# Modulation weights multiplied in the pauses of the norms, a reordered modulated input and an earlier first gain

## What is computed

```
h = h + 0.5 * rmsnorm(swiglu(rmsnorm(h, g[0]), w_gu, w_down), g[1])
xn = rmsnorm(h, g[2]);  z = xn @ w_in            # mLSTM, spatial gating, cross attention, gates
h = h + rmsnorm((g0*(y_m@w0) + g1*(y_s@w1) + g2*(y_x@w2)) @ w_out, g[3])
h = h + 0.5 * rmsnorm(swiglu(rmsnorm(h, g[4]), w_gu2, w_down2), g[5])
```

## Time and profile before

| what | value |
|---|---|
| runs shown | 3615.26, 3619.67, 3625.52 us |
| execution that was profiled | 3617.66 us |
| its span, first to last instruction | 3615.5 us |
| mean granted TensorE clock | 0.944 |
| TensorE busy | 3258.3 us, 90% |
| VectorE busy | 1895.6 us, 52% |
| ScalarE busy | 1405.6 us, 39% |
| GpSimd busy | 356.6 us, 10% |

### The profile page before, as it was taken

How to read it: one execution, slowest core, us unless ns; L and a number is a source line. 1 busy time by engine, 2 the same in 40 slices (tenths; PEclk the granted TensorE clock), 3 DMA queues, 4 the chain that set the end, 5 groups by cost and what they waited for, 6 DMA issues and landing times.

```text
span 3615.5 us, 54646 instructions
## 1 busy us (share of the span) xinstructions
PE 3258.3 (90%) x22888; PEld 2787.4 (77%) x22888; DVE 1895.6 (52%) x2581; ACT 1405.6 (39%) x2037; POOL 356.6 (10%) x387
## 2 busy tenths in 40 slices
PE   7989999898998999989898689898899979896897
PEld 7878887697887788779676578886688868786795
DVE  4356645445445664544524666663333367576554
ACT  3345554335335544433522333331323244412443
POOL 2000000100100000010010233330000001033000
PEclk9999999899999999999999789998899989987999
DMA  9655545665765555476441000002232223500464
GB/s 266 213 155 167 165 150 177 205 210 173 246 197 159 163 170 151 160 235 198 145 127 41 1 2 8 2 3 82 72 99 94 88 71 88 146 1 12 135 180 133
DMA packets 449227, 459.77 MB, mean 127 GB/s; under 512 B 18288, under 2 KB 347184, under 8 KB 449008
## 3 DMA queue, kind: packets, MB, share of 16 engines
q1 hardware_dynamic: 428624, 385.08, 35.8%
q0 software_dynamic: 20384, 71.52, 5.9%
HBM read 455.50 MB, written 1.05 MB: 126 GB/s over the span
## 4 chain that ended last, share of the span: by engine, by line
PE 75%; DVE 15%; ACT 5%; issue 4%; DMA 1%; POOL 1%; DVEq 0%; ACTq 0%; SPq 0%; POOLq 0%
PE banks L311 20%; PE banks L312 19%; PE banks L313 19%; PE banks L1901 2%; DVE weights_lo L297 1%; PE banks L4275 1%; PE banks L3518 1%; PE banks L3520 1%; PE banks L3499 1%; PE banks L1287 1%; DVE arena L3921 1%; DMA arena<-in_ada_w 1%; DVE first_input_split L1298 1%; PE banks L4246 1%; DVE arena L1430 1%
## 5 line engine op out<-in xcount | busy, mean ns | idle before, releaser
L297 DVE TENSOR_TENSOR weights_lo<-raw_weights,weights_hi 128x1024 fp32r<-128x1024 f32 (+2 forms) x399 | 472.7, 1186 | 544.7 <-ACT weights_hi L289 470.4
L289 ACT ACTIVATE weights_hi<-raw_weights 128x1024 fp32r<-128x1024 f32 (+2 forms) x399 | 409.3, 1027 | 530.5 <-PE banks L313 525.0
L262 DVE TENSOR_TENSOR weights_lo<-raw_weights,weights_hi 128x1024 fp32r<-128x1024 f32 x180 | 220.8, 1228 | 472.8 <-ACT weights_hi L255 285.2
L255 ACT ACTIVATE weights_hi<-raw_weights 128x1024 fp32r<-128x1024 f32 x180 | 190.4, 1060 | 516.9 <-PE banks L313 511.5
L311 PE MATMUL banks<-first_input_split,weights_hi 128*128 128x256 f32 (+1 forms) x1218 | 357.9, 294 | 9.1 <-DVE first_input_split L1298 5.2
L313 PE MATMUL banks<-first_input_split,weights_lo 128*128 128x256 f32 (+1 forms) x1218 | 347.9, 286 | 0.0
L312 PE MATMUL banks<-first_input_split,weights_hi 128*128 128x256 f32 (+1 forms) x1218 | 346.9, 285 | 0.0
L297 DVE TENSOR_TENSOR third_weights_split<-raw_weights,third_weights_split 128x1024 fp32r<-128x1024 f32 (+1 forms) x173 | 207.1, 1197 | 233.3 <-ACT third_weights_split L289 190.9
L311 PE MATMUL banks<-work_split,weights_hi 128*128 128x512 f32 (+2 forms) x776 | 272.2, 351 | 24.0 <-DVEq L2405 20.2
L312 PE MATMUL banks<-input_split,weights_hi 128*128 128x512 f32 (+2 forms) x776 | 270.6, 349 | 0.0
L313 PE MATMUL banks<-work_split,weights_lo 128*128 128x512 f32 (+2 forms) x776 | 270.4, 349 | 0.0
(11 more groups left out here) (597 smaller groups left out, 7169.2 us busy)
## 6 DMA issues: line engine op xcount, KB each, us to landing
raw_weights<-in_w_ffn_gu SPq DMA_DIRECT2D x176, 512.0 KB, 4.7
raw_weights<-in_w_in SPq DMA_DIRECT2D x144, 512.0 KB, 3.7
raw_weights<-in_mlp_w SPq DMA_DIRECT2D x128, 512.0 KB, 3.9
arena<-in_ada_w POOLq DMA_DIRECT2D x96, 512.0 KB, 6.7
raw_weights<-in_w_ffn_down SPq DMA_DIRECT2D x80, 512.0 KB, 3.4
raw_weights<-in_w_branch SPq DMA_DIRECT2D x48, 512.0 KB, 3.6
raw_weights<-in_ssd_w_in SPq DMA_DIRECT2D x48, 512.0 KB, 3.9
raw_weights<-in_w_mkv SPq DMA_DIRECT2D x32, 512.0 KB, 4.2
```

Of the source, the lines that this page charges most:

```text
L255: last = s.activation(self.w_hi[:, u % 2, :], self.raw[:, u, :], ACT.Copy)
L262: last = v.tensor_tensor(self.w_lo[:, u % 2, :], self.raw[:, u, :], self.w_hi[:, u % 2, :].bitcast(F32), ALU.subtract)
L289: last = s.activation(hi, raw, ACT.Copy)
L297: last = v.tensor_tensor(lo, raw, hi.bitcast(F32), ALU.subtract)
```

## The change

Modulation pieces: nine slots beside the stream, each transfer also waits until the stream has come to where it was emitted (`c.multiplied`), 3, 3, 2 and 3 groups are multiplied beside the four feed-forwards (44 pieces), and 52 pieces are multiplied right behind the last matmul of a stream, ahead of the norms: 12, 8, 12, 12 and 8 pieces at five places. Three of each twelve are brought into the rows of the hidden activations that are used up, the eights into buffers of the mixing branches. The sums of up to three groups are then taken together, at the beginning of the next side generator, from banks 6 and 7; `normed_input` turns its rows in banks 0 to 3. The first gain is issued ahead of the constants, the second and third behind the memory. `modulated_input` is put in another order, and the first product of the hybrid mixer waits for its input tile by tile.

```diff
-MOD_SLOTS = 5
+MOD_SLOTS = 9
+MOD_ARRIVALS = 12
...
-            pe.wait_ge(self.steps_done, at)
+            pe.wait_ge(self.steps_done, at - 1 if tiles_made else at)
...
         def product(banks, u, hi, lo, pe):
             for n, t in enumerate(tiles):
+                if waits:
+                    pe.wait_ge(*waits.pop(0))
...
-        feature_major(c, ch, c.y[:, t, :], x, t, 4 + 2 * t)
+        feature_major(c, ch, c.y[:, t, :], x, t, 2 * t)
...
-    mod_rows, pick = cols(z, GATES, 2, SEQ), cols(c.small, 448, 2, 2)
+    mod_rows, pick = cols(z, LD_AT + P, 3, SEQ), cols(c.small, 448, 2, 2)
...
+    def bring_modulation_weights(at, *free):
...
+            if used or m >= MOD_ARRIVALS:
+                g.wait_ge(c.mods_multiplied, max(used + [m - MOD_ARRIVALS]) + 1)
+            g.dma_start(cols(z, at, 2, BANK), src).then_inc(c.mods_arrived[m % MOD_ARRIVALS], 16)
...
+    def modulation_sums():
...
+        count = pieces // UNITS - first
...
+        @c.block.scalar
+            for i in range(count):
+                last = s.activation(mod_rows[:, i, :], c.ps[:, 6 + i // 2, i % 2 * SEQ:(i % 2 + 1) * SEQ], ACT.Copy)
...
+    def modulation_groups(beside, ahead):
+        free = [chain_end(ch) for ch in c.tile + [c.side]]
+        first, end = c.mods_brought, c.mods_brought + UNITS * beside + ahead
+
+        def bring_some():
+            while c.mods_brought < min(end, c.mod_pieces + MOD_SLOTS):
+                at = MOD_AT + (c.mods_brought - first) % MOD_SLOTS * UNIT
+                bring_modulation_weights(at, (c.multiplied, c.units_split - 1), *(free if at == MOD_AT else ()))
+                yield
+                yield
+        for _ in range(beside):
+            for u in range(UNITS):
+                yield from bring_some()
+                multiply_modulation()
+                yield
+            yield from modulation_sums()
+        yield from bring_some()
+
+    def more_modulations(stream, count):
+        rows = stream.todo[-1][0]
+        for i in range(count):
+            bring_modulation_weights(i * UNIT, (c.lo_made, rows.numbers[4 * i + 3] + 1 + UNITS))
...
+        for i in range(4):
+            bring_modulation_weights(V_TOK + i * UNIT, chain_end(ch))
...
-    slots[0].fill(g[0, 0, :])
-    slots[1].fill(g[0, 1, :])
-    slots[2].fill(g[0, 2, :])
...
     bring_memory()
+    slots[1].fill(g[0, 1, :])
+    slots[2].fill(g[0, 2, :])
...
+        memory = itertools.chain(modulation_sums(), memory_input(layer), params_needed() if layer == 0 else (),
+                                 modulation_groups(3 - layer, MOD_SLOTS + 3))
...
+        more_modulations(stream, 3)
+        multiply_modulations()
         stream = mixing
         add_normed(c, done, slots[1], 0.5)
...
+    try_root(c)
+    if stream:
+        stream.split_ahead(2)
+    else:
+        c.split_first_weights()
+    first = min(tiles, 3)
+    for t in range(first):
+        squared(t, chains[t])
+    for t in range(first):
+        normed(t, chains[t])
+    modulated(0, chains[0])
+    for t in range(first, tiles):
+        squared(t, chains[t])
+        normed(t, chains[t])
+    for t in range(1, tiles):
+        modulated(t, chains[t])
+        parts(t - 1, chains[t - 1])
+    parts(tiles - 1, chains[tiles - 1])
+    c.tiles_made = chain_ends(chains)
...
+        c.slots[0].fill(a["norm_g"][0, 0, :])
         make_constants(c)
```

## The result

The changed kernel takes 3567.68 us at the median of four runs (3559.80 to 3571.59), beside 3621.03 us of the kernel before: a ratio of 0.9854, with a 95% interval of 0.9835 to 0.9873. It is 53 us faster than before, and 30 us slower than I forecast. The profiled execution took 3568.06 us, its span is 3566.3 us against 3615.5: 49.2 us of the 81.4 that my sum had.

What follows compares the result with a forecast made beforehand. TensorE, busy 90% of the span, was taken as the bound. Terms 39.5 + 2 + 12.8 + 5.1 + 6 + 3 + 13 = 81.4 us left 3536.3 of the profiled 3617.7; with 2 us for the median, 3538 us, range 3518 to 3566.

Steps and rivals of the forecast that it cites:

- 52 pieces out of the streams: Feed-forward streams: 52 of 96 pieces, 0.76 us each, move into pauses that hide them; 39.5 us saved.
- sums, at full clock: Small matmuls of 24 groups: 13 groups batched in five, one restart per batch; 2 us saved, bounds 0 to 4.
- stalls in the feed-forwards: Start of each feed-forward: TensorE's waits for the first piece vanish because nine are issued ahead; 12.8 us saved.
- clock in the product stages: First block's products: less time at 1.2 GHz, 5.1 us behind first pieces plus 6 us behind pauses.
- start: Kernel start: first gain issued earlier brings the first matmul forward; 3 us saved, bounds 1.5 and 4.
- first modulated input: Ahead of the second block's first product: reordered tiles save 4 us, taking input tile by tile 3 us; 7 in all.
- The overrun rival: Pauses: the clock falls within them, twelve pieces take 12 or 13 us and delay transposes; 3560 us, chance 0.17.
- the modulated inputs: Four modulated inputs: new order and tile-by-tile start save 7, 4, 2 and 0.4 us; 13 in all, bounds 7 and 17.
- The slower rival: Feed-forwards: pieces reach TensorE before their weights, 44 stalls of 3.2 us; 3692 us, chance 0.03.
- I take 6 us from the three twelves and nothing from the eights: Products behind the five pauses: filled pauses recover 6 us of clock loss behind twelve pieces, none behind eight; bounds 0 and 15.
- The 5.1 us behind the first pieces: Feed-forwards: removing first-piece stalls recovers 1.7 us of lowered clock behind each of three; 5.1 us saved.
- The row at 634.53: Profile row: a 2.89 us pause, transposes and another 2.05 us pause sufficed for a low clock; cited against full clock recovery.

Runs made afterwards that it cites:

- the control: The changed kernel once more with only an empty line added, nothing altered: 3560.23 us, ratio 0.9834 to the kernel before.
- the slower pace: Changed kernel with a piece beside a stream emitted every one and a half weight units instead of every unit: 3549.10 us, ratio 0.9811.
- the combination: Changed kernel plus identity transposes at both idle places of the pauses, sums some five units later, a piece every one and a half units: 3532.31 us, ratio 0.9770.

## Why the prediction was right and wrong

All in the first block, the spans of before against those of the changed kernel; the term of the pieces is what is left of the 37.5 us when the others are taken out, so an error of any other term of the product stages lies in it too:

| term | forecast | measured | read from |
|---|---|---|---|
| 52 pieces out of the streams | 39.5 | 41.4, or 0.80 each | remainder; 42 by the feed-forwards of the kernel with all pieces in the streams (37.0, plus 9.1 of clock and 0.8 of idle, less 4.5 of sums) |
| sums, at full clock | 2 | -0.7 | 24 x 0.81 = 19.4 before, 11 single ones (8.9) and 11.2 after |
| stalls in the feed-forwards | 12.8 | 7.8 | idle 21.0 us before, 13.2 after |
| idle in the mixings | 0 | -0.4 | 19.35 and 19.7 |
| clock in the product stages | 11.1 | -10.6, in the control -7.3 | half of 71.4 - 50.2, or of 64.7 - 50.2 |
| pauses | 0 | 0.3 | five 1.1 shorter, one 0.8 longer |
| start | 3 | 2.1 | 19.80 to 17.69 |
| first modulated input | 7 | 10.7 | 30.19 to 19.49 |
| sum, first block | 75.4 | 50.6 | 1816.74 to 1766.17 |
| second block | 6.4, taken as 6 in the sum | -1.4, in the control 5.5 | 1798.8 to 1800.1 or 1793.2 |

*Right.* The pieces: both the price in a stream and that the pause hides them. The overrun rival is out, with 2.1 to 3.5 us left behind the pieces in the changed kernel, though the time that it forecast, 3560 us, is what the control measured: that is a coincidence. The wait for first pieces went whole. By the distances from last to first product the modulated inputs gave 16.1 us where I had 13, the first 10.7 of it; the stream behind the first got only 0.6 us longer (143.8 to 144.4), so its early start is nearly all gain. The start gave 2.1, inside its bounds and nearer to the 2 us that I had worked out beside my 3 by the Trainium skill ("DMA: Bandwidth & Descriptors", Queues, rings and completion order). The slower rival did not come: no piece is late.

*Wrong, and the step of it.* "I take 6 us from the three twelves and nothing from the eights; bounds 0 and 15". The term of the clock is 22 us off, most of the 25 missing in the first block. Some 16 of them lie behind the three twelves, where 9.7 us more are missing instead of 6 less (17.2 against 7.5). The sign lay outside my bounds: I took it for certain that more work in a pause can only help. The 5.1 us behind the first pieces can't be told apart in this sum: those stalls are gone, but the stall at 944.94 has a low stretch of its own. The run with all pieces in the streams and the three with filled pauses show what holds. What counts for the next stream is where in time the clock falls. Twelve pieces of 5.4 us put off the fall from 3 to 5 us behind the last product to 9, so that the next stream bears it. The 2 us of idle between the transposes and the first product, which I named and left alone, decide. The row at 634.53, from which I argued that the clock would hardly come back, was the right row; I drew from it only that the gain would be small. The Trainium skill ("TensorE: Matmul & The Clock Gate", Part 1) has it that the low clock is the default and activity lifts it. With both idle stretches filled the traces agree (1.00 in five windows of the combination); a pause filled with twelve pieces only, with 2 to 3 us left empty on both sides of the transposes, came out worse than an empty one (17.2 us missing behind three, against 5.0 or 7.5).

*Also mis-sized.* The batches of sums: emitted "in the first two units of the next stream", two of them stand in just that low stretch and take 4.97 us each instead of 2.6, and at full clock a batch of 24 costs 2.6, so nothing is saved beside three times 0.81. The stalls: I had "nine units lie between issue and use" for the pieces, and did not ask what nine pieces issued at 2.87 us each do to the weights beside them. One stall of 3.34 us with 3.4 us at 1.2 GHz behind it is what shows, and the slower pace gives 8 to 16 us. The rest, 7 us in the second block of the first profile, is variation between executions.

*Luck.* The first measurement lies 2 us above my range and the control, the same kernel, 6 us inside it. That second number says nothing for the reasoning: the clock term had the wrong sign in both profiles, and the range was wide enough to hide it.

*Open.* Whether the small matmuls themselves bring the clock down (the falls behind three batches of 24) was not tried alone: in the combination, with the batches five units later, there was none behind them, with more filling there were two again, and with the batches late and no filling there was one. The first feed-forward also gains 4.4 us from the slower pace; its idle (4.3 to 2.0 us) and low clock (8.6 to 5.8 us, half of it lost) come to 3.7. How much the filling ahead of the transposes is worth, and whether the parts of the combination add up, is open too.

## What to carry to other kernels

Work moved into a pause was free in time here, but it moves the pause's fall of the clock too: look at the granted clock of the 15 us behind the pause, and fill the last idle stretch ahead of the products first. A batch of tiny matmuls right behind a pause pays double if the clock is low there (4.97 us against 2.6). Before more buffers let transfers run ahead, add up what all streams ask for while the buffers fill, and pace the issues to what is left over.

## What the runs showed that I had not expected

- Pieces of eight records back to back take 0.45 us each, beside products they cost 0.76 to 0.80.
- Behind the three pauses with 5.4 us of work in them 17.2 us of full speed were missing, behind the same pauses empty 5.0 (7.5 in the kernel before), behind filled ones, with the sums later, 0.
- Thirteen transposes of the identity, 1.6 us of work whose result nobody reads, make the kernel 16 to 23 us faster, in the five pauses and at the start.
- The same 12460 matmuls of the second block took 1793.2 and 1800.1 us in two executions of one kernel, and 1789.8 to 1803.7 over twelve profiles.
